# A one-core transformer layer with 16 experts: the search for each expert's 66 best tokens split into two halves, and three weight transfers placed behind a store of normed rows

## The reference, cut to what matters

```python
xn = rms_norm(h, norm2_g)
cap = 2 * T // 16                                   # 66
logits = einsum('btd,de->bte', xn, w_router)
aff = softmax(logits, axis=-1)
gate, idx = top_k(swapaxes(aff, 1, 2), cap)         # per expert: its 66 best tokens
xe = xn[idx]
hid = silu(xe @ w_gate) * (xe @ w_up)               # 16 experts, 1024 -> 2048
ye = (hid @ w_down) * gate[..., None]
h = h + zeros_like(h).at[idx].add(ye)
out = rms_norm(h, final_norm_g)[:, 16:]
```

## Time and profile before

| | us |
|---|---|
| median of 3 runs | 1794.79 |
| lowest and highest | 1794.64, 1796.58 |
| the profiled execution | 1796.06 |
| its span, first to last instruction | 1794.2 |
| PE busy in the span | 1499.7 (84%) |
| DVE busy | 1305.5 (73%) |
| ACT busy | 1024.3 (57%) |
| POOL busy | 324.9 (18%) |
| mean DMA rate over the span | 270 GB/s |

### The profile page before, as it was taken

How to read it: one execution, slowest core, us unless ns; L and a number is a source line. 1 busy time by engine, 2 the same in 40 slices (tenths; PEclk the granted TensorE clock), 3 DMA queues, 4 the chain that set the end, 5 groups by cost and what they waited for, 6 DMA issues and landing times.

```text
span 1794.2 us, 43227 instructions
## 1 busy us (share of the span) xinstructions
PE 1499.7 (84%) x19619; PEld 1158.3 (65%) x19619; DVE 1305.5 (73%) x806; ACT 1024.3 (57%) x663; POOL 324.9 (18%) x180
## 2 busy tenths in 40 slices
PE   7899999999999999667887778768768876876874
PEld 5466766877888887567665646656565664665552
DVE  5746656665533336769998998888899889889974
ACT  4333432435422234468776777787677777777773
POOL 1154154324100000310740111110011011011100
PEclk9799999999999999779999999899889989989997
DMA  9202202330055521669999999999999999999993
GB/s 358 84 1 83 71 1 94 95 95 24 25 219 180 167 95 60 274 238 378 407 404 401 414 407 406 403 416 409 398 415 410 401 409 409 407 398 416 423 397 109
DMA packets 109689, 484.32 MB, mean 270 GB/s; under 512 B 6043, under 2 KB 51419, under 8 KB 92908
## 3 DMA queue, kind: packets, MB, share of 16 engines
q1 hardware_dynamic: 103728, 467.19, 66.1%
q0 software_dynamic: 5040, 14.10, 2.9%
q10 hardware_dynamic: 844, 1.89, 0.3%
HBM read 470.24 MB, written 12.91 MB: 269 GB/s over the span
## 4 chain that ended last, share of the span: by engine, by line
DMA 37%; PE 34%; DVE 14%; ACT 7%; issue 3%; POOL 3%; SPq 1%; ACTq 0%; POOLq 0%; DVEq 0%
PE ps_all L1319 24%; DMA slot<-in_w_exp_gate 17%; DMA slot<-in_w_exp_down 17%; DVE wl L1255 11%; ACT wh L775 6%; PE ps_all L1435 3%; PE ps_all L1342 2%; DMA raw<-in_w_in 2%; PE ps_all L1423 1%; PE ps_all L1478 1%; DMA xn_rows<-xb 1%; DMA h_rows<-ye,tok 1%; DVE wsp L913 1%; POOL psp L470 0%; POOL psp L468 0%
## 5 line engine op out<-in xcount | busy, mean ns | idle before, releaser
L1255 DVE SCALAR_TENSOR_TENSOR wl<-slot,wh 128x4096 f16<-128x4096 f32 x184 | 809.8, 4423 | 97.9 <-ACT wh L775 97.7
L775 ACT ACTIVATE wh<-slot 128x4096 f16<-128x4096 f32 x184 | 664.5, 3616 | 229.3 <-DMA slot<-in_w_exp_down 103.0
L1648 PE MATMUL ps_all<-xcur,wl 128*128 128x66 f16 x4096 | 424.2, 198 | 186.2 <-ACT sg L781 108.1
L1648 PEld LDWEIGHTS ps_all<-xcur,wl 128*128 128x128 f16 x4096 | 398.9, 103 | 200.4 <-ACT sg L781 106.5
L1649 PE MATMUL ps_all<-xcur,wh 128*128 128x66 f16 x4096 | 424.0, 199 | 5.2 <-issue 5.2
L1650 PE MATMUL ps_all<-xcur,wh 128*128 128x66 f16 x4096 | 423.7, 201 | 1.6 <-issue 1.6
L1649 PEld LDWEIGHTS ps_all<-xcur,wh 128*128 128x128 f16 x4096 | 399.0, 101 | 4.7 <-issue 4.5
L1650 PEld LDWEIGHTS ps_all<-xcur,wh 128*128 128x128 f16 x4096 | 399.1, 101 | 1.6 <-issue 1.6
L1319 PE MATMUL ps_all<-xnt,wsp 128*128 128x272 f16 (+1 forms) x2688 | 312.6, 279 | 6.1 <-ACT acc L601 4.3
L1319 PEld LDWEIGHTS ps_all<-xnt,wsp 128*128 128x128 f16 x2688 | 265.2, 99 | 54.5 <-issue 9.3
L1662 PE MATMUL ps_all<-wh,hidt 128*66 128x512 f16 x480 | 181.8, 379 | 21.5 <-DVE wl L1255 21.3
(11 more groups left out here) (244 smaller groups left out, 1637.0 us busy)
## 6 DMA issues: line engine op xcount, KB each, us to landing
slot<-in_w_exp_gate SPq DMA_DIRECT2D x64, 2048.0 KB, 23.9
slot<-in_w_exp_up SPq DMA_DIRECT2D x64, 2048.0 KB, 21.6
slot<-in_w_exp_down SPq DMA_DIRECT2D x64, 2048.0 KB, 22.8
raw<-in_w_in SPq DMA_DIRECT2D x32, 1024.0 KB, 6.2
raw<-in_w_ret_out SPq DMA_DIRECT2D x4, 1024.0 KB, 12.1
raw<-in_w_hy_out SPq DMA_DIRECT2D x4, 1024.0 KB, 8.4
raw<-in_w_o SPq DMA_DIRECT2D x4, 1024.0 KB, 5.1
win_t<-in_c_win SPq DMA_DIRECT2D x2, 1536.0 KB, 10.2
```

Source lines behind the costliest of these rows:

```text
L775: nc.scalar.activation(wh[c % RING][:, :], slot[(c + 2) % SLOTS][:, :], ACT.Copy, scale=W_S).then_inc(S["w_hi"], 1)
L1255: nc.vector.scalar_tensor_tensor(wl[c % RING][:, :], slot[(c + 2) % SLOTS][:, :], W_S, wh[c % RING][:, :], ALU.mult, ALU.subtract).then_in ...
L1648: nc.tensor.matmul(dst, lo, xcur[:, k, 0, :], start=k == 0 and t % TIL == 0, stop=False, skip_group_check=True)
```

## The change

The search. PE no longer transposes the softmax into 16 x 528; it multiplies a wider tile lgw (128 x 5 x 80, zero but for columns 32 to 47) with the identity, so that the first 272 tokens come to partitions 0 to 15 and the last 256 to partitions 32 to 47. DVE copies this to work (48 x 272) in two copies, and the nine rounds run over 272 elements. The result is two sorted lists of 66 per expert. The copies of indices and values for the second list are made backwards, so that after the transposes element r of the one stands beside element 65 - r of the other, and the larger of each pair is one of the 66 best. Nine small DVE instructions take the place of four. The values' copies are made by ACT, ahead of its waits for the h_rows stores. POOL clears four tiles once the logits are done.

The weights. SP waits for x_store[3], the fourth store of normed rows, before it issues units 4 and 5. No other instruction of SP moves, but expert 1's first load stands behind these in SP's line.

```diff
+T_A = 16 + 2 * 128
...
             sp.wait_ge(S["tile_done"], AT[("WO", KD - 1)] + 1)
+            sp.wait_ge(x_store[3], 16)
             load_first(4)
             load_first(5)
...
                 nc.gpsimd.tensor_tensor(sqa[:, :], sqa[:, :], sqt[:, :], ALU.add).then_inc(S["sq_sum"], 1)
+            pool.wait_ge(S["lg_done"], KD)
+            nc.gpsimd.memset(lgw[:, :, :], 0.0).then_inc(S["sel_clear"], 1)
+            nc.gpsimd.memset(work[:, T - T_A:T_A], -1.0).then_inc(S["sel_clear"], 1)
+            nc.gpsimd.memset(valf[:, :], 0.0).then_inc(S["sel_clear"], 1)
+            nc.gpsimd.memset(idxf[:, :], 0.0).then_inc(S["sel_clear"], 1)
             pool.wait_ge(S["g2_row"], 16)
...
+            act.wait_ge(S["vals_out"], 1)
+            act.wait_ge(S["sel_clear"], 4)
+            nc.scalar.activation(valf[0:E, 0:CAP], vals[0:E, 0:CAP], ACT.Copy).then_inc(S["picked_v"], 1)
+            nc.scalar.activation(valf[32:48, 0:CAP], vals[32:48, CAP - 1::-1], ACT.Copy).then_inc(S["picked_v"], 1)
             for i in range(3):
                 act.wait_ge(h_store[i], 16)
...
-            nc.vector.tensor_copy(work[:, :], full(3, 0, E)).then_inc(S["work_in"], 1)
-            dve.wait_ge(S["work_in"], 1)
+            nc.vector.tensor_copy(work[:, 0:T - T_A], ps_all[0:48, 3584:3584 + T - T_A]).then_inc(S["work_in"], 1)
+            nc.vector.tensor_copy(work[0:E, T - T_A:T_A], ps_all[0:E, 3584 + T - T_A:3584 + T_A]).then_inc(S["work_in"], 1)
+            dve.wait_ge(S["work_in"], 2)
             for r in range(ROUNDS):
...
-            nc.vector.tensor_copy(idxf[:, :], idxu[:, :]).then_inc(S["idx_found"], 1)
-            dve.wait_ge(S["idx_found"], 1)
+            nc.vector.tensor_copy(idxf[0:E, 0:CAP], idxu[0:E, 0:CAP]).then_inc(S["idx_found"], 1)
+            nc.vector.tensor_copy(idxf[32:48, 0:CAP], idxu[32:48, CAP - 1::-1]).then_inc(S["idx_found"], 1)
             j = AT[("C",)]
             dve.wait_ge(S["tile_done"], j + 1)
-            nc.vector.tensor_copy(tok[:, :], ps_all[0:CAP, 3584:3584 + E]).then_inc(S["cols_in"], 1)
-            nc.vector.tensor_scalar(gate[:, :], ps_all[0:CAP, 3584 + E:3584 + 2 * E], 1.0 / (W_S * HID_S), None, ALU.mult).then_inc(S["cols_in"], 1)
+            nc.vector.tensor_copy(sel[:, 0:48], ps_all[0:CAP, 3584:3632]).then_inc(S["picked"], 1)
+            nc.vector.tensor_scalar(sel[:, 48:96], ps_all[0:CAP, 3632:3680], 1.0 / (W_S * HID_S), None, ALU.mult).then_inc(S["picked"], 1)
+            dve.wait_ge(S["picked"], 2)
+            nc.vector.scalar_tensor_tensor(pick[:, 0:E], sel[:, 0:E], -float(T_A), sel[:, 32:48], ALU.add, ALU.subtract).then_inc(S["picked"], 1)
+            nc.vector.tensor_tensor(pick[:, E:2 * E], sel[:, 48:48 + E], sel[:, 80:96], ALU.is_ge).then_inc(S["picked"], 1)
+            nc.vector.tensor_tensor(gate[:, :], sel[:, 48:48 + E], sel[:, 80:96], ALU.max).then_inc(S["cols_in"], 1)
+            dve.wait_ge(S["picked"], 4)
+            link(nc.vector.tensor_tensor(pick[:, 0:E], pick[:, 0:E], pick[:, E:2 * E], ALU.mult))
+            nc.vector.scalar_tensor_tensor(tok[:, :], pick[:, 0:E], float(T_A), sel[:, 32:48], ALU.add, ALU.add).then_inc(S["cols_in"], 1)
...
             for k, (s0, p) in enumerate(TS):
-                last = nc.tensor.transpose(pair(3, P0 + s0, P0 + s0 + p, E), lgs[0:p, k, :], ident[0:p, 0:p])
+                part = lgw[0:p, k, 32:80] if s0 < T_A else lgw[0:p, k, 0:48]
+                at = 3584 + (s0 if s0 < T_A else s0 - T_A)
+                last = nc.tensor.matmul(ps_all[0:48, at:at + p], part, ident[0:p, 0:p], start=k == 0, stop=k == NT - 1, skip_group_check=True)
...
-            pe.wait_ge(S["work_in"], 1)
-            pe.wait_ge(S["idx_found"], 1)
-            for a, src in enumerate((idxf, vals)):
-                last = nc.tensor.transpose(ps_all[0:CAP, 3584 + E * a:3584 + E * a + E], src[:, 0:CAP], ident[0:E, 0:E])
+            pe.wait_ge(S["work_in"], 2)
+            pe.wait_ge(S["idx_found"], 2)
+            pe.wait_ge(S["picked_v"], 2)
+            for a, src in enumerate((idxf, valf)):
+                last = nc.tensor.transpose(ps_all[0:CAP, 3584 + 48 * a:3584 + 48 * a + 48], src[:, 0:CAP], ident[0:48, 0:48])
```

More of the change, by code:

```diff
@@ L157, in job_list @@
         if i == 1:
-            add(("AT",), "work_in", 1)
+            add(("AT",), "work_in", 2)
     add(("C",), "cols_in", 2)
@@ L184 @@
         LAST_JOB.append(AT[("WO", 2 * (_n - C_O) + 1)])
[L186 to L196, removed]
+SEMS = ("ident_in consts g2_in filt_params dft_fwd dft_inv win tables w4_in xt_saved x_again g2_row gf_row out_stored sq_dve ones_set "
+        "eps_set warm rms1_sq rms1_root rms1_inv x_raw rb_ready x_scaled x_hi x_lo_d x_lo_p border conv_w wr_ready raw_hi raw_lo tile_done "
+        "filt_arg filt_red sin_ready u_evac u_used w4_ready filt_win filt_hi filt_lo g_odd g_fold g_mid z_fold zt_hi zt_split z_skip z_mul "
+        "p_sub p_sum p_hi p_lo y_done yb_prod yb_hi dec_exp dec_ln mask_arg mask_ready rot_mul rot_ready qk_hi qk_lo v_hi v_lo sc_ready "
+        "sc_hi sc_lo sq_ready sq_both rms_root silu_ready og_ready yain_prod yain_hi yain_split gate_ready mix_a mix_b mix_sum mix_hi "
+        "mix_split h_add hh_hi hh_lo sq_part sq_sum lg_done ss_done ht_evac xr_ready sel_clear vals_out picked picked_v rms2_root rms2_inv "
+        "xn2_ready logits_in lg_sub lg_exp lg_aff work_in idx_found cols_in x_in xe_done chain w_hi w_lo xcur_hi xcur_lo chunk_used "
+        "psum_free hidt_hi hidt_lo ye_ready rows_landed fin_sq fin_root fin_ready").split()
 def build(nc, A, out, xt_rows, xn2_rows, h_rows):
@@ L236, in build @@
         lsum = sb("lsum", [128, NT], F32, SM + 2784)
-        vals = sb("vals", [E, 8 * ROUNDS], F32, SM + 2816)
-        idxu = sb("idxu", [E, 8 * ROUNDS], U32, SM + 3104)
-        idxf = sb("idxf", [E, 8 * ROUNDS], F32, SM + 3392)
+        vals = sb("vals", [48, 8 * ROUNDS], F32, SM + 2816)
+        idxu = sb("idxu", [48, 8 * ROUNDS], U32, SM + 3104)
+        idxf = sb("idxf", [48, 8 * ROUNDS], F32, SM + 3392)
+        lgw = sb("lgw", [128, NT, 80], F32, XN + 16384)
+        work = sb("work", [48, T_A], F32, XN + 16384 + 1600)
+        valf = sb("valf", [48, 8 * ROUNDS], F32, XN + 16384 + 2688)
+        sel = sb("sel", [CAP, 96], F32, XN + 16384 + 3008)
+        pick = sb("pick", [CAP, 2 * E], F32, XN + 16384 + 3392)
         gate = sb("gate", [CAP, E], F32, SM + 3904)
@@ L261, in build @@
         g2b = sb("g2b", [128, D], F32, FREE + 8192)
-        work = sb("work", [E, T], F32, XN + 16384)
         ybin = sb("ybin", [128, KD, 2, T], F16, YB)
@@ L1224, in _ @@
             link(nc.vector.reciprocal(lsum[:, :], lsum[:, :]))
-            nc.vector.tensor_tensor(lgs[:, :, :], lgs[:, :, :], lsum[:, :].unsqueeze(2).to_broadcast([128, NT, E]),
+            dve.wait_ge(S["sel_clear"], 4)
+            nc.vector.tensor_tensor(lgw[:, :, 32:32 + E], lgs[:, :, :], lsum[:, :].unsqueeze(2).to_broadcast([128, NT, E]),
                                     ALU.mult).then_inc(S["lg_aff"], 1)
@@ L1229, in _ @@
             dve.wait_ge(S["tile_done"], j + 1)
-            nc.vector.tensor_copy(work[:, :], full(3, 0, E)).then_inc(S["work_in"], 1)
-            dve.wait_ge(S["work_in"], 1)
+            nc.vector.tensor_copy(work[:, 0:T - T_A], ps_all[0:48, 3584:3584 + T - T_A]).then_inc(S["work_in"], 1)
+            nc.vector.tensor_copy(work[0:E, T - T_A:T_A], ps_all[0:E, 3584 + T - T_A:3584 + T_A]).then_inc(S["work_in"], 1)
+            dve.wait_ge(S["work_in"], 2)
             for r in range(ROUNDS):
                 v8, i8 = vals[:, 8 * r:8 * r + 8], idxu[:, 8 * r:8 * r + 8]
-                link(nc.vector.max(v8, work[:, :]))
+                ins = nc.vector.max(v8, work[:, :])
+                if r == ROUNDS - 1:
+                    ins.then_inc(S["vals_out"], 1)
+                    dve.wait_ge(S["vals_out"], 1)
+                else:
+                    link(ins)
                 link(nc.vector.max_index(i8, v8, work[:, :]))
```

## The result

| | before | after |
|---|---|---|
| median of 13 runs, us | 1794.79 | 1800.63 |
| lowest and highest | 1791.56, 1799.35 | 1797.29, 1803.46 |
| span of the profiled execution | 1794.2 | 1799.9 |

The ratio is 1.003, with a 95% interval from 1.0021 to 1.0039: **slower by 5.4 us, between 3.8 and 7.0** (the two medians differ by 5.8). The prediction was 3.7 us slower, 1798.5 us.

A forecast was written before the change was run, and what follows sets the result against it. The first fetch's landing, held by late rows, was taken to set when the full weight stream starts. Landing at 776.7 instead of 772.98 us adds 3.7 to 1794.79, giving 1798.5 us; range 1790.5 to 1801.5 us.

The forecast's parts named there:

- rival C: Last store takes a full tile's 12.4 us and the fetch lands at 777.3 to 779: +4.3 to +6 us; chance 0.13.
- What binds: Before the first fetch, the rows come last, by 1.7 us, not the search; the shorter search alone is worth 0.
- The search: DVE's 26 steps take 7.0 us less; rounds end at 757.4 us, gate and tok at about 760.5, 4.7 us earlier.
- The rows: Without weights in the way, stores land sooner; x_store[3] is issued at 755.05 us and lands at 757.95.
- The weights stand in the way of what POOL issues next: Held units delay last store, gfb and fetch: 7.15 MB take 17.7 us, fetch lands at 776.7 us, +3.7 us.
- The last store: The last normed store, an eighth of a tile, takes 4.5 us beside the weights; up to about 11 the sum stays.
- B: POOL's transfers get their share and the fetch lands at 769.9 us: -3.1 us, 1790.7 to 1791.7 us; chance 0.18.
- D: No change: the weight units have less lead and two queues share; fetch lands at 774.5 to 775.8, +1.5 to +2.8 us; chance 0.20.
- E: Search steps on DVE cost no less at 272 elements; search ends at 767.5, 1798.5 us or a little more; chance 0.03.
- From the landing to the end: From the first fetch's landing to the kernel's end, the distance stays that of before, 1021.2 us.

The follow-up runs named there:

- e1: The changed kernel without SP's wait, so the halved search alone; ratio 0.9994 to the kernel before.
- e2: The kernel before with SP's wait for the fourth normed store alone, old search kept; ratio 1.0017 to the kernel before.
- e7: The kernel before with SP's wait for the fourth normed store alone, measured a second time; ratio 1.0034 to the kernel before.
- e11: The changed kernel with expert 1's first unit issued only after the first fetch has landed; ratio 1.0005 to the kernel before.
- e3: The changed kernel with gfb (the final norm's row) loaded after the first fetch is issued, not before; ratio 1.0018 to the kernel before.
- e6: The changed kernel with units 4, 5 and expert 1's first unit all held until the first fetch has landed; ratio 1.0003 to the kernel before.
- e4: Halved search, units 4 and 5 issued at once, expert 1's first unit alone held until the first fetch has landed; ratio 0.9981 to the kernel before.
- e12: Halved search with expert 1's first unit alone held until the first fetch has landed, measured again; ratio 0.9974 to the kernel before.
- e5: Halved search, unit 4 at once, unit 5 and expert 1's first unit after the first fetch's landing, gfb after its issue; ratio 0.9987 to the kernel before.
- e10: The kernel before, old search kept, with expert 1's first unit alone held until the first fetch has landed; ratio 0.9985 to the kernel before.

## Why the prediction was right, and where a size was off

The direction and the mechanism held. The size was off: 5.4 us by the ratio lies above the forecast's own +3.0 to +4.6, and the median of 1800.63 us is in the stated range only through its upper end, which was set for rival C. (That end is 1800.8 + 0.95 = 1801.75 us; the text has 1801.5.)

- **What binds.** That the rows and not the search come last held: e1 is level with the kernel before.
- **The search.** 0.43 us a step held (436 and 427 ns). The small DVE instructions are eleven for four, nine for three without the copies to work. The wider products on PE took 2.2 us in place of 1.1 (I took 0.5 more), and the rounds ended at 758.13 instead of 757.4, tok at 760.68 as put (760.5). That ACT's copies stand behind stores I costed at nothing; under the hold that is so, without it they take back most of the gain (e1).
- **The rows.** x_store[3] was issued at 755.44 (755.05) and landed in 3.0 us; SP passed at 758.49 (758.0). Of this 0.4 us is the stretch beginning later.
- **The weights stand in the way of what POOL issues next.** Held, and it is the whole loss (e2, e7, e11). The term that was mis-sized is where the lot ends. I had 17.7 us after a start of 1.0, hence 776.7; the last unit landed at 760.06 + 18.7 = 778.8 and the fetch 0.5 us behind it. 0.5 us of the difference is the later start. Most of the rest is at the end of the transfer, where my sum ran at full rate to the last byte. Four-microsecond windows of the changed kernel:

```profile
758.00:762.00 4.00, 0.34 (x2) 0.19 (x2) 2.06 (x10) 2.96 (x2) 1.46 (x2) 0.50 0.73 231
762.00:766.00 4.00, 0.00 (x0) 0.00 (x0) 0.00 (x0) 0.82 (x1) 0.00 (x0) 0.50 1.01 428
...
774.00:778.00 4.00, 0.00 (x0) 0.00 (x0) 0.00 (x0) 0.00 (x0) 0.00 (x0) 0.50 0.78 301
```

The first moves 231 GB/s, 1.7 us short of 404, of which my 1.0 us and the later start are 1.5. In the last the engines' share has fallen to 0.78, and from 777.5 to 778.5 us 0.02 MB are moved, before the final unit lands: the engines don't end together. So the fetch is +6.3 us where I had +3.7 (+5.9 counted from the reference store), and the time +5.4.
- **The last store** took 6.46 us, I gave 4.5; as the text said, it did not matter to the sum.
- **The rivals.** B (POOL's transfers get their share) is out: the fetch landed at 779.24 us, not 769.9. 0.5 MB less in front of the fetch in POOL's queue (e3) brought it 1.7 us earlier, 2.1 MB less in SP's (e11) 5.8. Packets, MB and engines' share by queue in the changed kernel, 766 to 770 us (the first line) and 770 to 774 us, q1 being SP's queue and q0 POOL's:

```profile
q1 hardware_dynamic: 106, 1.70, 99.4%
q1 hardware_dynamic: 92, 1.28, 79.0%
q0 software_dynamic: 93, 0.38, 24.9%
```

  gfb was issued at 766.29, and POOL's queue moved no packet before 770; beside no weights, in the kernel before, its first packets came within 1.5 us. From then on the queues moved equal numbers of packets, SP's some 14 KB each and POOL's 4, so POOL had 23% of the bytes where B had half. In the kernel before, 750 to 753 us, three queues moved 51, 51 and 54. That is turns by packet, as the prediction quotes them. C's size, +4.3 to +6, was reached, but not by its mechanism: the last store landed at 765.7, not 771.2. The fetch took 11.74 us, as the 11.8 of the earlier trace rows. D (the fetch lands at 774.5 to 775.8) and E (steps that cost no less) are out by the landing and by the 0.43 us.
- **From the landing to the end** it took 1020.7 us (1021.2 before), the fixed distance that the prediction rested on. e6, 1029.2, showed that it is fixed only while the held units land before the engines want them. It is not exact either: e4 and e12 are one kernel and have 1023.6 and 1021.2, e2 has 1018.1, e5 1024.6.

## What to carry to other kernels

A large prefetch in the same DMA engines delays small transfers that are issued behind it from another queue: here a fetch took 11.74 us in place of 4.24, a store of 64 KB 6.46 in place of 2.18. How long depends on what the prefetch still has to move; that store landed 13 us ahead of the prefetch's last unit, the fetch half a microsecond behind it. Holding it back only helps if the small transfers that matter are then done before it is released: release it after the last of them, and hold no more than fits into the time left before it is wanted. And before a step is made faster, see what the next instruction still waits for: here 7 us of search were worth nothing alone, and, with other waits gone, about 1 us in the fetch's landing (e4 and e12 against e10), which the times don't resolve.

## What the runs showed of the hardware that was not expected

A small DVE step is drawn out to the end of a multiply that POOL has begun. In e4 the second cast of the indices, 0.19 us in the changed kernel's timeline, began just after POOL did:

```profile
757.95 2.33 POOL L522 TENSOR_TENSOR xb<-xb,g2b 16x1024 f32<-16x1024 f32 x1
758.02 2.31 DVE L1258 CAST idxf<-idxu 16x66 f32<-16x66 uint32 x1
```

It ends at 760.33, POOL's at 760.28. In the kernel before, the cast's 0.73 us ended at 764.47 in the same way; in the changed kernel the 0.80 us end at 758.96, POOL's multiply at 758.91; in e1 it was a step with two inputs. The nine rounds beside the same multiplies were not slowed. In e1 the two casts, begun at 758.11 and 758.33, ahead of POOL's at 758.35, took 0.18 us each; and a step with two inputs, begun 0.01 us behind POOL's next multiply (762.14 and 762.13), still took 0.17. The Trainium skill, SBUF — State Buffer, section "Who interferes with whom", says that the pair of ports which VectorE and GpSimd share is an exclusive lock, held for the instruction, which copies and casts may take and which a step with two SBUF inputs needs beside a GpSimd step that reads. The trace agrees but for that last step, which stays open. Here it was worth up to 2.1 us to the search, and none to the kernel.

The other is the landing of small transfers beside large ones. The Trainium skill, DMA: Bandwidth & Descriptors, section on queues, rings and completion order, says that a DMA's completion is a write that lands only after every earlier write of that engine, across its queues. No run here shows that rule at work: the fetch lands 0.5 us behind the last unit in the changed kernel, but 0.9 us ahead of it in e3 and 2.5 behind in e11, and the last store, issued after units 4 and 5, landed at 765.7 us, ahead of both (766.3 and 771.5). What the runs do show is the late start and the turns by packet told above.
